# Recurrence's output gate by seven products for all heads, and the forward scan ahead of the state steps

## The reference

```
x += 1/2 * postnorm(SwiGLU(prenorm(x)))                  half-step FFN 1
h  = prenorm(x); z = h @ W_in                            all projections of the mixer
  A: dilated window attention, three groups of 8 heads
  B: HGRN2, 8 heads, expansion 128, chunks of 64 tokens, both directions
       q = silu(qz); v = iz; f = lb + (1 - lb) * sigmoid(fz); k = 1 - f; b = cumsum(log f)
       a = tril((q e^(b-ref)) (k e^(ref-b))^T);  o = a v + (q e^b) state
       state_n = decay_n * state_(n-1) + (k e^(b_last-b))^T v
       o = (o_fwd + o_bwd) * rsqrt(mean(o^2) + eps) * norm_w;  o = o * silu(gz)
  y = (sig(gA) * (A @ P_A) + sig(gB) * (B @ P_B)) @ W_out
x += postnorm(y)
x += 1/2 * postnorm(SwiGLU(prenorm(x)))                  half-step FFN 2
```

## Time and profile before

| | |
|---|---|
| median of three runs | 1442.38 us |
| span of the profiled execution | 1440.1 us |
| difference of the two | 2.3 us |
| PE busy | 1432.0 us, 99% |
| DVE busy | 903.9 us, 63% |
| ACT busy | 669.5 us, 46% |
| POOL busy | 23.3 us, 2% |
| loads of weight blocks, time to landing | 3.5 us median, 512 KB each |
| chain that ended last | PE 98% |

### The profile page before, as it was taken

The page is one execution under the profiler, slowest core; times in us unless marked ns, Lnnn a source line. Parts: engine busy times, 40 slices in busy tenths (PEclk is TensorE's granted clock), DMA queues, the critical chain, the costliest instruction groups (busy, mean ns, idle before and its releaser), DMA issues.

```text
span 1440.1 us, 21210 instructions
## 1 busy us (share of the span) xinstructions
PE 1432.0 (99%) x8104; PEld 1226.9 (85%) x8104; DVE 903.9 (63%) x1424; ACT 669.5 (46%) x1083; POOL 23.3 (2%) x43
## 2 busy tenths in 40 slices
PE   9999999999999999999999999999999999999998
PEld 7899999888898888888888888888889888888886
DVE  7988875335753455567866766664548555564975
ACT  5455555334542546555446554553445333233542
POOL 0000000000100000000000000000000000000000
PEclk9999999999999999999999999999999999999999
DMA  6333323423332323225332122224331243323753
GB/s 198 117 118 107 99 89 118 131 89 132 96 110 89 91 74 88 64 74 169 114 99 74 58 87 65 68 72 131 104 103 45 88 149 99 101 88 116 243 183 131
DMA packets 44317, 153.71 MB, mean 107 GB/s; under 512 B 5287, under 2 KB 5287, under 8 KB 44240
## 3 DMA queue, kind: packets, MB, share of 16 engines
q1 hardware_dynamic: 41472, 143.67, 31.5%
q0 software_dynamic: 2624, 8.95, 2.0%
q10 hardware_dynamic: 144, 0.04, 0.0%
HBM read 147.63 MB, written 4.23 MB: 105 GB/s over the span
## 4 chain that ended last, share of the span: by engine, by line
PE 98%; DMA 1%; ACT 0%; DVE 0%; issue 0%; SPq 0%; DVEq 0%; ACTq 0%
PE ps L470 22%; PE ps L471 21%; PE ps L472 21%; PE ps L620 4%; PE ps L621 4%; PE ps L622 4%; PE ps L1679 2%; PE ps L1681 2%; PE ps L1680 2%; PE ps L2508 1%; PE ps L2078 1%; PE ps L2079 1%; PE ps L2080 1%; PE ps L2891 1%; PE ps L2488 1%; PE ps L2911 1%
## 5 line engine op out<-in xcount | busy, mean ns | idle before, releaser
L470 PE MATMUL ps<-hh,whi 128*128 128x512 f32 x976 | 385.9, 395 | 0.8 <-DVE wlo L2006 0.4
L472 PE MATMUL ps<-hh,wlo 128*128 128x512 f32 x976 | 380.2, 390 | 0.0
L471 PE MATMUL ps<-hl,whi 128*128 128x512 f32 x976 | 380.2, 390 | 0.0
L416 DVE TENSOR_TENSOR wlo<-raw,whi 128x1024 fp32r<-128x1024 f32 x172 | 210.5, 1224 | 250.4 <-ACT whi L411 250.2
L411 ACT ACTIVATE whi<-raw 128x1024 fp32r<-128x1024 f32 x172 | 181.8, 1057 | 380.9 <-PE ps L472 356.3
L470 PEld LDWEIGHTS ps<-hh,whi 128*128 128x128 f32 x976 | 183.1, 188 | 44.9 <-issue 3.9
L472 PEld LDWEIGHTS ps<-hh,wlo 128*128 128x128 f32 x976 | 183.2, 188 | 38.7
L471 PEld LDWEIGHTS ps<-hl,whi 128*128 128x128 f32 x976 | 183.3, 188 | 36.4
L470 PE MATMUL ps<-ah,whi 128*128 128x512 f32 (+1 forms) x192 | 71.5, 372 | 0.0
L472 PE MATMUL ps<-ah,wlo 128*128 128x512 f32 (+1 forms) x192 | 71.3, 371 | 0.0
L471 PE MATMUL ps<-al,whi 128*128 128x512 f32 (+1 forms) x192 | 71.3, 371 | 0.0
(11 more groups left out here) (564 smaller groups left out, 2978.8 us busy)
## 6 DMA issues: line engine op xcount, KB each, us to landing
raw<-in_wstream SPq DMA_DIRECT2D x190, 512.0 KB, 3.5
w_raw<-in_wstream SPq DMA_DIRECT2D x32, 512.0 KB, 4.3
ring<-in_wstream SPq DMA_DIRECT2D x20, 512.0 KB, 4.3
xt<-in_x_t SPq DMA_DIRECT2D x16, 256.0 KB, 4.6
raw_early<-in_wstream SPq DMA_DIRECT2D x8, 512.0 KB, 4.3
raw_late<-in_wstream SPq DMA_DIRECT2D x4, 512.0 KB, 3.8
x_dram<-x_tok POOLq DMA_DIRECT2D x4, 512.0 KB, 4.1
x_tok<-x_dram POOLq DMA_DIRECT2D x4, 512.0 KB, 5.6
```

Source lines behind the costliest of these rows:

```text
L416: nc.vector.tensor_tensor(wlo[:, s, :], raw[:, s, :], whi[:, s, :].bitcast(F32), ALU.subtract).then_inc(split_done, 1)
L470: nc.tensor.matmul(out, w, m, start=start, stop=False)
L471: nc.tensor.matmul(out, w, ml, start=False, stop=False)
L472: return nc.tensor.matmul(out, wl, m, start=False, stop=stop)
```

## The change

Three things change together.

The gate leaves the turn. `gh_tok` = h @ W_gh is made for all heads right behind the value projection, by the same seven products in a second round over the same token sums (28 blocks instead of 14 in the stage). The order within a round is new: the steps that need sums of weights come in another order, the first token block's sums leave through PSUM (ACT copies the bank pair U into Z, on which t1 goes on), and the loads have semaphores of their own (8 loads a round, the sums in places of their own). `gh_tok` takes the place of `xt`: POOL stores `xt` to DRAM before and loads it back when the last gate has been read; the norm behind the mixer waits for it (`x_parked`).

A turn has three projections, in the order ff, fb, q. The three blocks of a head alternate between the two places over two heads (`head_block`). ACT applies Silu to the head's part of `gh_tok` and DVE multiplies the output with the inverse root and the gate in one operation for each of four token tiles, before the transposes; behind them ACT takes the high part straight from PSUM with the norm's weight as scale, and DVE the low part.

In DVE's list of a turn, scan, keys and rel of the forward direction stand ahead of the 14 state steps; those of the backward direction behind them. In ACT's list the exponentials of both directions stand ahead of the squares of the output, and the Silu of q at the end of the turn, behind them, where it stood at the beginning; the keys' products come ahead of the queries' products.

The core of the diff (a line "..." marks what is left out):

```diff
-          ("gate_a", 6), ("ih", 7), ("hgrn", 2 * GH_HEADS + 2), ("gate_h", KT - 2), ("w_out", KT // 2),
+          ("gate_a", 6), ("ih", 14), ("hgrn", 3 * GH_HEADS // 2 + 2), ("gate_h", KT - 2), ("w_out", KT // 2),
...
+IH_STEPS = tuple((x, c) for x in ("b11", "b21", "t2", "t3", "t1", "t4", "b22") for c in range(2))
...
+            for r in range(2):
+                if r:
+                    ih_tail(dve, r, 0)
+                    ih_tail(dve, r, 1)
+                    c12(r - 1)
+                ih_tail(dve, r, 2)
+                if r == 0:
+                    h_sums_tail(dve, 2)
+                for part, c in IH_SUMS[:2]:
+                    ih_sum(dve, r, part, c)
+                ih_tail(dve, r, 3)
+                if r == 0:
+                    h_sums_tail(dve, 3)
+                for part, c in IH_SUMS[2:4]:
+                    ih_sum(dve, r, part, c)
+                ih_tail(dve, r, 4)
+                ih_tail(dve, r, 5)
+                if r:
+                    dve.wait_ge(sem("x_parked"), 16)
+                c11(r)
+                ih_sum(dve, r, "c", 0)
+                ih_tail(dve, r, 6)
+                ih_sum(dve, r, "c", 1)
+                ih_tail(dve, r, 7)
+                ih_sum(dve, r, "b", 0)
+                ih_tail(dve, r, 8)
+                ih_sum(dve, r, "b", 1)
+                ih_tail(dve, r, 9)
+                ih_tail(dve, r, 10)
+                ih_tail(dve, r, 11)
+                c22(r)
+                ih_tail(dve, r, 12)
+                ih_tail(dve, r, 13)
+                c21(r)
...
+        def head_block(two, parity, b):
+
+            k = 3 * parity + b
+            return FIRST["hgrn"] + 3 * two + k // 2, k % 2
...
                         for t in range(TT):
                             last = nc.tensor.transpose(ps[:, 2 + d, t * P:(t + 1) * P],
                                                        k_in[d][:, t * P:(t + 1) * P], ident)
                         last.then_inc(sem(f"kh_turned{d}"), 1)
+                    pe.wait_ge(sem("q_in0"), h)
+                    pe.wait_ge(sem("q_in1"), h)
-                project_part(1, ("gate_done", h) if scan else None)
+                project_part(1, ("sig_q", h) if scan else None)
...
-                project_part(2, ("sig_q", h + 1))
+                project_part(2, ("sig_f0", h + 1))
...
-                project_part(3, ("sig_f0", h + 1))
+                if not own:
+                    project_part(3, ("sig_f1", h + 1))
...
+            def next_head(two, parity, b):
+                pair, s = head_block(two, parity, b)
+                head(act, pair - 1, s)
 
             def b_head(h):
 
...
+                act.wait_ge(sem("o_turned"), h)
+                nc.scalar.activation(bh[:, bass.ds(h - 1, 1), :].rearrange("p a n -> p (a n)"), ps[:, 5, :],
+                                     ACT.Copy, scale=par[:, 40:41]).then_inc(sem("bh_done"), 1)
+
+            def turn(two, parity, scan, finish, own=True):
+                h = 2 * two + parity
+                banks = [head_block(0, parity, b)[1] for b in range(4)]
+                next_head(two, parity, 2)
+                if own:
+                    nc.scalar.activation(sig[0][:], ps[:, banks[0], :], ACT.Tanh, scale=0.5).then_inc(sem("sig_f0"), 1)
+                else:
+                    nc.scalar.activation(first_gates[0], ps[:, banks[0], :], ACT.Sigmoid).then_inc(sem("sig_f0"), 1)
                 if scan:
                     for d in range(2):
                         act.wait_ge(sem(f"kh_turned{d}"), h)
...
                                              ACT.Copy).then_inc(sem("kh_out"), 1)
                 if finish:
                     b_head(h - 1)
...
+                next_head(two, parity, 3)
+                if own:
+                    nc.scalar.activation(sig[1][:], ps[:, banks[1], :], ACT.Tanh, scale=0.5).then_inc(sem("sig_f1"), 1)
+                else:
+                    nc.scalar.activation(first_gates[1], ps[:, banks[1], :], ACT.Sigmoid).then_inc(sem("sig_f1"), 1)
+                if scan:
+                    if finish:
+                        act.wait_ge(sem("o_norm"), TT * (h - 1))
+                    nc.scalar.activation(gate_tok, gh_tok[:, :, bass.ds((h - 1) * P, P)], ACT.Silu
+                                         ).then_inc(sem("gate_done"), 1)
                 nc.scalar.preload_act_table_set("natural_log_exp_and_others")
                 if own:
                     for d in range(2):
...
                         act.wait_ge(sem(f"sig_f{d}"), h + 1)
                         nc.scalar.activation(cum[d][:], sig[d][:], ACT.Ln, scale=half_oml[:, lane],
                                              bias=lb_mid[:, lane]).then_inc(sem("logf"), 1)
+                    for d in range(2):
+                        act.wait_ge(sem("rel"), 2 * h + d + 1)
+                        nc.scalar.activation(e_up[d][:], k_in[d][:], ACT.Exp).then_inc(sem(f"e_up{d}"), 1)
+                        nc.scalar.activation(e_dn[d][:], k_in[d][:], ACT.Exp,
+                                             scale=-1.0).then_inc(sem(f"e_dn{d}"), 1)
+                    for d in range(2):
+                        nc.scalar.activation(e_ref[d][:], both(cum[d][:])[:, :, REF[d]], ACT.Exp
+                                             ).then_inc(sem(f"e_ref{d}"), 1)
+                next_head(two, parity, 4)
                 if scan:
                     act.wait_ge(sem("o_psum"), h + 1)
                     for t in range(TT):
...
                                          bias=eps[:]).then_inc(sem("o_ln"), 1)
                     act.wait_ge(sem("o_ln"), h)
                     nc.scalar.activation(o_rs[:], o_rs[:], ACT.Exp, scale=-0.5).then_inc(sem("o_rstd"), 1)
+                nc.scalar.preload_act_table(ACT.Silu)
                 if own:
...
+                    if scan:
+                        act.wait_ge(sem("q_in1"), h)
+                    nc.scalar.activation(q_h[:], ps[:, banks[2], :], ACT.Silu).then_inc(sem("sig_q"), 1)
                 else:
...
+                    nc.scalar.activation(first_gates[2], ps[:, banks[2], :], ACT.Sigmoid).then_inc(sem("sig_q"), 1)
+                    next_head(two, parity, 5)
+                    nc.scalar.activation(first_gates[3], ps[:, banks[3], :], ACT.Sigmoid).then_inc(sem("sig_g"), 1)
...
+            def keys_in(h, d):
 
                 dve.wait_ge(sem(f"e_up{d}"), h + 1)
...
                 dve.wait_ge(sem(f"e_dn{d}"), h + 1)
                 nc.vector.tensor_tensor(k_in[d][:], key[d][:], e_dn[d][:], ALU.mult).then_inc(sem(f"k_in{d}"), 1)
+
+            def queries_in(h, d):
+
+                nc.vector.tensor_tensor(q_in[d][:], q_h[:], e_up[d][:], ALU.mult).then_inc(sem(f"q_in{d}"), 1)
...
             def b_tail(h):
                 dve.wait_ge(sem("bh_done"), h)
                 one = bass.ds(h - 1, 1)
...
+                nc.vector.scalar_tensor_tensor(out=bl[:, one, :].rearrange("p a n -> p (a n)"), in0=ps[:, 5, :],
+                                               scalar=par[:, 40:41],
+                                               in1=bh[:, one, :].rearrange("p a n -> p (a n)").bitcast(F32),
+                                               op0=ALU.mult, op1=ALU.subtract).then_inc(sem("bl_done"), 1)
+
+            def decays(h, d):
+
+                flip = slice(None, None, -1) if d else slice(None)
+                lane = bass.ds(d * GH_HEADS + h, 1)
+                dve.wait_ge(sem("logf"), 2 * h + d + 1)
+                nc.vector.tensor_tensor_scan(out=cum[d][:, flip], data0=keep_state[d][:, flip],
+                                             data1=cum[d][:, flip], initial=0.0, op0=ALU.mult,
+                                             op1=ALU.add).then_inc(sem("cum"), 1)
+                nc.vector.tensor_scalar(key[d][:], sig[d][:], minus_half_oml[:, lane], half_oml[:, lane],
+                                        ALU.mult, ALU.add).then_inc(sem("keys"), 1)
+                dve.wait_ge(sem("cum"), 2 * h + d + 1)
+                nc.vector.tensor_tensor(both(k_in[d][:]), both(cum[d][:]),
+                                        both(cum[d][:])[:, :, REF[d]:REF[d] + 1].to_broadcast([P, NC_CH, C]),
+                                        ALU.subtract).then_inc(sem("rel"), 1)
+
+            def turn(two, parity, scan, finish, own=True):
+                h = 2 * two + parity
+                next_tail(two, parity, 2)
                 if finish:
...
+                    b_tail(h - 1)
                 if scan:
                     dve.wait_ge(sem("att_psum"), h)
 
...
                     nc.vector.copy_predicated(att[:], tri.unsqueeze(2).to_broadcast([P, 2, TT, C]).bitcast(U32),
                                               ps[:, 4, :].rearrange("p (d t c) -> p d t c", d=2, c=C)
                                               ).then_inc(sem("att_out"), 1)
...
+                next_tail(two, parity, 3)
                 if scan:
                     dve.wait_ge(sem("att_out"), h)
```

(69 more changed lines are left out.)

438 lines of the change are left out of this document (189 added, 249 removed).

## The result

The changed kernel takes 1465.45 us (median of five runs, 1464.47 to 1467.58), the kernel before, run beside it, 1442.25 us: 1.58% slower, ratio 1.0158 (1.0146 to 1.0171). Forecast were 1460, a range of 1447 to 1470 and, within it, 1456 to 1465 with a chance of 0.64: the time lies in the range and just above the inner one. The profiled execution has a span of 1463.9 us where 1457.6 was the sum. It took 1465.69 us, so its time lies 1.8 us above its span, where the prediction had added 2.3; that is most of why the loss is 23.2 us in medians and 23.8 us in spans.

A forecast was written before the change was run, and what follows sets the result against it. PE's list of products was taken to bound the kernel. -5.5 + 19.5 + 2.0 + 1.5 = +17.5 us on the span of 1440.1 gave 1457.6; the median lies 2.3 above, so 1460, range 1447 to 1470.

The forecast's parts named there:

- What bounds the kernel: Whole kernel: as long as PE's list of products, so fewer products shorten it while every operand comes in time.
- What PE gains: Gate's block leaves eight turns (43.6 us), a second round of seven products comes in (38.1 us): net 5.5 us less.
- The wait at the states: State products in turns 1 to 7: PE waits 1.96 us because DVE does the forward scan, keys and rel first.
- The wait at the attention products: Later in turns 1 to 7: PE waits another 0.77 us for q; with the states' wait, 19.5 us over seven turns.
- the sign named in the prediction: Profile after: attention products wait for q_in eight times, 0.8 us, and 2 in the first turn.
- The first turn: Turn without state steps or gate: PE waits for the q products, loss 2.0 us.
- The value stage: Value projection's first round: eight DVE operations between splits 1 and 4 make PE wait, loss 1.5 us.
- The clock: Rival: waits lower the granted clock, one projection in each of seven turns 5.45 us longer, +38, 1498 us; chance 0.04.
- late weights: Value projection's first round: first sum waits 1 us for weights, loss 2.5; a reason to widen the range to 1470.
- the parked transfers: Residual's DMA out and back, up to 16 us each way, costed at nothing; a reason to widen the range to 1470.
- Table loads: Two loads in each turn's chain, no drain counted; rival with a drain of 1.38 each: 19 us more, 1479; chance 0.02.
- Parking the residual: Storing the residual to DRAM and fetching it back, 2 MB each way on POOL's queue: taken as 0.

The follow-up runs named there:

- the kernel with the chain cut: Changed kernel with state steps ahead of both scans, att_sum ahead of the next block's split, third split and gate's Silu later: 1440.41 us, ratio 0.9985.
- the kernel with the states first: Changed kernel with the forward scan, keys and rel put back behind the 14 state steps, nothing else: 1452.58 us, ratio 1.0070.
- The fillers: Unused matmuls in PE's wait for the states: 8 in the changed kernel, 1461.10 us; 18 in the kernel with both scans ahead, 1472.15 us.
- the kernel with both scans ahead: Changed kernel with the backward scan, keys and rel also put ahead of the state steps: 1488.4 us, ratio 1.0322.

## Why the prediction was right, and what it mis-sized

**What bounds the kernel.** Right: PE's list. With one block less and nothing waiting a turn takes 23.74 us (the kernel with the chain cut), 23.72 by the sum.

**What PE gains, -5.5.** Right; no block of the second round costs other than 2.72.

**The wait at the states.** Counted 1.96, measured 1.95 in the row and 13.7 over seven. That it fits so closely is in part luck: the states are done 10.08 behind zero, 0.20 before the 10.28 counted, and PE goes on 0.26 behind that, which was counted at nothing. The cause is shown from three sides: the scan taken away from in front of the states removes the wait, a second one doubles it, and 0.5 us less in front of the logarithm makes it 1.5.

**The wait at the attention products.** The chain was counted to reach them at 19.75; measured 19.65 and 19.57 in turns 1 and 2. In turns 1 and 2 PE waits 0.5 there, not 0.77, and the turns take 26.4 and 26.3 where 26.5 were counted. In turns 3 to 7 there is no wait, since the lower clock makes PE itself late: 20.6. So the sign named in the prediction, eight such waits, did not come: there are three, with the first turn's. That a turn is a closed chain of ACT and DVE is shown by the kernel with the states first, which takes 25.35 where the measured 26.4 less the 1.1 us for which DVE waited ahead of the scan give 25.3.

**The first turn.** 2.0 counted, 2.3 measured. Hand-overs that I counted at nothing add up: behind the end of fb (765.59) the table load starts at 10.78 (10.63 counted) and the attention products at 14.14 (the queries' products were counted to end at 13.82).

**The value stage.** 1.5 counted, 2.0 measured. DVE split block 1 at 677.38 (677.35 counted) and block 4 at 687.99 (687.55): two of the weight sums wait 0.2 for the one before them, and the products after the wait start slowly (0.2 us in the block behind it). The transfers were no part of it: the row of SP has four of them within 1.75 us from 676.70, and neither PE nor DVE waits for a DMA in the first round's opening.

**The clock: the term that was mis-sized.** In the prediction it was a rival of 4%, priced at a whole projection a turn (38 us), and zero in the sum. It is neither. Behind a wait of 2 us the granted clock falls to 1.2 GHz in five of seven turns, costs 1.0 us each, and 1.5 behind the wait of 2.3 in the first turn: 6.5 us. The difference between 17.5 and 23.8 is 6.3; the errors of the other terms cancel to 0.2 (the value stage and the first turn were counted 0.8 too short, the seven turns 1.0 too long). My argument against it, that no row of before shows a fall between two products, was empty: before, PE had no wait of that length between products to show one behind. The section of the Trainium skill named there ("TensorE: Matmul & The Clock Gate", HAM oscillation) tells of longer waits than these; the trace has falls behind waits of 2 us, and the measurement decides. The fillers show that the clock is a cost and not only a sign, in two kernels (4.4 and 16 us). It is luck that these 6.5 us left the time inside the range: the upper end of 1470 was set for late weights and the parked transfers, and neither cost anything.

**Table loads.** As in the rows of before, the logarithm starts 1.30 us behind the load (870.27 to 871.57). The drain that the Trainium skill ("ScalarE: Activation LUTs", What ACT_TABLE_LOAD costs) adds to each switch is not to be seen in these rows, and the 1479 us that it would have given are out.

**Parking the residual.** At nothing, as taken: PE's waits name neither `xt` nor a DMA.

**Open.** Why the clock stays up behind the same wait in turns 1 and 2, and falls in 3 to 7, the runs don't tell; nor why it falls in the first turn of the changed kernel and not in that of the kernel with both scans ahead. The number of falls may also differ from run to run: of the five runs the fastest (1464.47 us) has a mean clock of 0.995 and the slowest (1467.58) 0.991, and only one of them was profiled.

## What to carry to other kernels

When the engine that bounds a kernel gets less to do, the chain through the others does not shrink with it: before the change, add up one period's chain from a result of that engine to the operand that it asks for next, and put it beside the new period. Busy shares don't show it (DVE 63% before and after); here the same operations in another order are worth 25 us. In such a chain anything that nobody waits for belongs behind what somebody waits for, and a wait on TensorE is to be priced with the slower clock behind it.

## What the runs showed of the hardware

TensorE's granted clock can fall in the work behind a wait of only 2 us, in a kernel that is otherwise dense: the 14 state products (28 instructions in the trace) then took 2.70 us in place of 1.68, and the first 5 us behind the wait held all of it. Whether it falls is not told by the wait alone: behind 2.0 us it fell in five turns of seven, behind 2.2 us in the first turn of five kernels, and not in that of the one with both scans ahead and no fillers. Behind waits of 4.2 us it fell in all seven turns, at 2.5 us a turn. Behind waits of 1.5 us (seven of them) and of 1.3 (one in each of two kernels) it did not fall. Useless matmuls in the wait kept it up in all seven turns of both kernels that had them.
